# Prompt attention scores: two heads side by side on the halves of the contraction, in place of zero-padded queries

## The reference

```python
# group A (x = 0): chunk band, 8 chunks of 64 to the left, with a bias by distance
sc = jnp.einsum('bcqhd,bckhd->bchqk', chunked(q), k_band) * (d ** -0.5)
sc = jnp.where(valid, sc + bias, -jnp.inf)
o = jnp.einsum('bchqk,bckhd->bcqhd', jax.nn.softmax(sc), v_band)
# group B (x = 1): the 256 keys that an indexer scores highest, for each query
_, idx = lax.top_k(isc, k_sel)
sc = jnp.einsum('bqhd,bqkhd->bhqk', q, kg) * (q.shape[-1] ** -0.5)
o = jnp.einsum('bhqk,bqkhd->bqhd', jax.nn.softmax(sc), vg)
```

## Time and profile before

| | |
|---|---|
| median of 3 runs | 2865.4 us (2864.28 to 2867.36) |
| the profiled execution: its time, its span | 2869.77 us, 2866.3 us |
| PE busy, share of the span | 2603.8 us, 91% |
| PEld busy | 2326.6 us, 81% |
| DVE busy | 1359.8 us, 47% |
| ACT busy | 992.7 us, 35% |
| POOL busy | 632.3 us, 22% |
| mean granted clock of PE | 0.963 |
| first prompt score to the last but one tile's end | 1324.2 to 1673 us of the span |

### The profile page before, as it was taken

How to read it: one execution, slowest core, us unless ns; L and a number is a source line. 1 busy time by engine, 2 the same in 40 slices (tenths; PEclk the granted TensorE clock), 3 DMA queues, 4 the chain that set the end, 5 groups by cost and what they waited for, 6 DMA issues and landing times. The chain is left out here.

```text
span 2866.3 us, 39971 instructions
## 1 busy us (share of the span) xinstructions
PE 2603.8 (91%) x16468; PEld 2326.6 (81%) x16468; DVE 1359.8 (47%) x2369; ACT 992.7 (35%) x1691; POOL 632.3 (22%) x470
## 2 busy tenths in 40 slices
PE   2799999999998999986998989989299999999998
PEld 2799999988887799975776766658289999998886
DVE  6423333234543598986777723332523232333544
ACT  4333333333332323233666532221333333323332
POOL 5444333300001021831000000000633344320000
PEclk9899999999998999987999989999699999999999
DMA  2122122266542121213000334551011221227553
GB/s 88 41 82 78 61 78 72 88 229 218 209 142 64 49 95 63 78 51 120 23 31 30 111 105 167 178 190 45 22 61 63 91 78 61 78 68 264 187 205 145
DMA packets 153108, 294.26 MB, mean 103 GB/s; under 512 B 14032, under 2 KB 90456, under 8 KB 152928
## 3 DMA queue, kind: packets, MB, share of 16 engines
q1 hardware_dynamic: 146688, 268.12, 27.6%
q0 software_dynamic: 6240, 23.59, 2.2%
HBM read 237.26 MB, written 61.78 MB: 104 GB/s over the span
## 5 line engine op out<-in xcount | busy, mean ns | idle before, releaser
L720 DVE TENSOR_TENSOR f_dl<-f_raw_d,f_dh 128x2048 fp32r<-128x2048 f32 x66 | 151.3, 2293 | 274.1 <-ACT f_dh L568 274.1
L568 ACT ACTIVATE f_dh<-f_raw_d 128x2048 fp32r<-128x2048 f32 x66 | 126.5, 1916 | 321.6 <-PE f_pV L151 287.4
L149 PE MATMUL f_pX<-f_xop,f_g_shi 128*128 128x256 f32 (+1 forms) x528 | 159.4, 302 | 21.6 <-ACT f_gh L499 21.6
L499 ACT ACTIVATE f_gh<-f_pX 128x256 f32<-128x256 f32 (+1 forms) x132 | 54.1, 410 | 352.8 <-PE f_pX L151 352.7
L1897 PEld LDWEIGHTS t_po<-t_v,t_pT 128*128 128x128 f32 x1056 | 135.2, 194 | 33.8 <-DVE t_osb L1621 14.2
L150 PE MATMUL f_pX<-f_xop,f_g_shi 128*128 128x256 f32 (+1 forms) x528 | 158.5, 300 | 0.0
L151 PE MATMUL f_pX<-f_xop,f_g_slo 128*128 128x256 f32 (+1 forms) x528 | 158.4, 300 | 0.0
L1754 ACT ACTIVATE t_sc<-t_sc,t_small 128x640 f32<-128x640 f32 (+8 forms) x136 | 100.0, 735 | 165.8 <-DVE t_small L1682 130.2
L150 PE MATMUL f_pX<-f_xop,f_u_shi 128*128 128x256 f32 (+1 forms) x528 | 156.3, 296 | 0.0
L151 PE MATMUL f_pX<-f_xop,f_u_slo 128*128 128x256 f32 (+1 forms) x528 | 156.3, 296 | 0.0
L149 PE MATMUL f_pX<-f_xop,f_u_shi 128*128 128x256 f32 (+1 forms) x528 | 156.3, 296 | 0.0
(11 more groups left out here) (329 smaller groups left out, 8131.7 us busy)
## 6 DMA issues: line engine op xcount, KB each, us to landing
f_raw_d<-in_ffn_w_down SPq DMA_DIRECT2D x66, 1024.0 KB, 4.9
hid<-f_gh SPq DMA_DIRECT2D x22, 1152.0 KB, 8.8
f_raw_h<-hid SPq DMA_DIRECT2D x66, 384.0 KB, 5.5
f_g_raw<-in_ffn_w_gate SPq DMA_DIRECT2D x22, 1024.0 KB, 5.4
f_u_raw<-in_ffn_w_up SPq DMA_DIRECT2D x22, 1024.0 KB, 6.4
proj<-w_stage POOLq DMA_DIRECT2D x12, 1152.0 KB, 5.6
i_raw<-in_w_in SPq DMA_DIRECT2D x12, 1024.0 KB, 5.2
f_x<-in_x_prompt SPq DMA_DIRECT2D x16, 512.0 KB, 6.3
```

Of the source, the lines that this page charges most:

```text
L149: pe.matmul(out, a[0], b[0], start=first, stop=False, skip_group_check=goes_on)
L499: act.activation(dst, by_tile(pX[:, c, 0:N[c]]), ACT.Copy).then_inc(s_copy, 1)
L568: act.activation(d_hi[slot(q)][:], raw_d[slot(q)][:], ACT.Copy).then_inc(s_dhi, 1)
L720: dve.tensor_tensor(d_lo[slot(q)][:], raw_d[slot(q)][:], d_hi[slot(q)][:].bitcast(F32), ALU.subtract)
```

## The change

Queries are kept without zeros, two heads to a slice as the keys are. The scores of an even and an odd head are issued together, each a matmul over the 64 partitions of its head: for each four blocks first the even, then the odd head. The order becomes: behind `turn(g)` with g odd come `score(g + 1)` and `score(g + 2)`, behind an even one none. DVE and ACT walk the same list. The copy to `qT` is one of 128 partitions in place of two of 64, and the memset goes.

```diff
         plan.append(("turn", g))
-        if g + 2 < len(heads):
-            plan.append(("score", g + 2))
+        if g % 2 and g + 1 < len(heads):
+            plan += [("score", g + 1), ("score", g + 2)]
         if g >= 1:
             plan.append(("value", g - 1))
...
-        qT = keep("qT", [P, 2, H, P], F32)
+        qT = keep("qT", [P, 2, HT, P], F32)
...
-            pool.memset(qT[:], 0.0).then_inc(s_zero, 1)
...
-                    pool.wait_ge(s_zero, 3)
+                    pool.wait_ge(s_zero, 2)
...
-            act.wait_ge(s_zero, 1)
...
-                    for r in range(2):
-                        i = act.activation(qT[r * HD:(r + 1) * HD, n % 2, r::2, :],
-                                           pm[r * HD:(r + 1) * HD, :].rearrange("p (f c) -> p f c", c=P), ACT.Copy, scale=HD ** -0.5)
-                    i.then_inc(s_ma, 1)
+                    act.activation(qT[:, n % 2, :, :], pm[:].rearrange("p (f c) -> p f c", c=P), ACT.Copy, scale=HD ** -0.5).then_inc(s_ma, 1)
...
-                elif e[0] == "score":
+                elif e[0] == "score" and e[1] % 2 == 0:
...
                     if g >= 2:
-                        pe.wait_ge(s_mx, g - 1)
+                        pe.wait_ge(s_mx, g)
                     for c in range(0, nb, 4):
                         c1 = min(c + 4, nb)
-                        last = pe.matmul(ps[g % 2][:, c * P:c1 * P], qT[:, (x * NP + t) % 2, h, :],
-                                         kT[x][:, h // 2, (k0 + c) * P:(k0 + c1) * P], start=True, stop=True)
-                    last.then_inc(s_s, 1)
+                        for r in range(2):
+                            rs = slice(r * HD, (r + 1) * HD)
+                            last = pe.matmul(ps[r][:, c * P:c1 * P], qT[rs, (x * NP + t) % 2, h // 2, :],
+                                             kT[x][rs, h // 2, (k0 + c) * P:(k0 + c1) * P], start=True, stop=True)
+                            if c1 == nb:
+                                last.then_inc(s_s, 1)
```

## The result

The median went from 2865.6 to 2982.5 us (four executions each): ratio 1.0407, interval 1.0389 to 1.0425, +117 us. The forecast was slower, 2904, with a range to 2942: the sign was right and the size a third of what came. An execution over 1.5% longer than the fastest of its kernel is left out of ratios and medians; this concerns two of the four of one experiment, halves alone.

The account below looks back on a forecast made before the run. PE was taken to bound the kernel. Tiles of nb = 5 (+25 us) and the others (+3.8, +3.7, -2, +8.4) sum to +39: 2909 on the profiled execution, 2904 as median, range 2885 to 2942.

Parts of the forecast that it names:

- PE bounds the kernel before: Prompt attention loop: PE goes without a gap at nb = 5, 2.69 us a head, with slack of 1.5 us elsewhere.
- Overlap: Pair's scores on PE: only odd head's first record beside even head's second; 1.50 us for 2.14 at nb = 5, saving 34.
- The bound of 56 us of streaming: Upper bound on PE's saving from overlapping a pair's scores: half of all score streaming; 34 us was taken.
- the sum on PE: PE's score saving against array changes: -34 + 26 = -8 us; with full doubling 26 - 56 = -30.
- Array changes: PE going from 128 rows to 64 and back once a pair: 0.4 us each, 26 us for 64 pairs.
- Closed loop: Pair's chain through PE, DVE and ACT, no lookahead: 6.95 us at nb = 5 against 5.38; with overlap, chance 0.52.
- The sum: Change in prompt attention's time, tile by tile over all nb: +39 us, 2909 on the profiled execution.
- Prep: Preparing a tile at nb = 5: key copy stands behind the odd head's exponential; 2.1 us charged for `prep`.
- The clock: Rival: PE's idle gaps drop half the stretch to 1.2 GHz, about 0.7 us a pair, +45 us, 2949; chance 0.17.
- the two gaps of 1 us: PE's waits in a pair at nb = 5: some 0.8 us ahead of the even head's turn, 1.1 ahead of the odd's.
- my signs of being wrong: Odd head's turn starting without waiting, stretch clock under 0.9, or 64-row weight loads taking other than 0.19 us.
- the absence of overlap: Rival: the pair's score halves run one after the other, +23 us more at nb above 4: +62, 2927; chance 0.20.

Follow-up runs that it names:

- halves alone: The changed kernel with the old order, one head at a time in 64 rows: 3036 us from the two shorter executions, ratio 1.059.
- the two opened kernels: Early pair scores, key and query rows of `prep` separated, earlier `out`, output scaled between adds: 2817.6 us with 64-row halves, 2842.0 with zero-padded 128 rows.
- prep split: Kernel before, with `prep`'s query rows transposed behind the turn and next score, and no DVE select half at h = 2: 2840.5 us, 0.9914.
- the opened kernel with halves: Changed kernel with scores behind the even turn, `prep` in two parts, earlier `out`, output scaled between the adds: 2817.6 us, 0.9824.
- the small matmuls of 64 rows: Kernel before, with one matmul of 64 rows and 4 columns ahead of each head's scores: 2950.2 us, 1.0283.
- halves alone with prep split: One head at a time in 64 rows, old order, `prep`'s query rows later, no select half at h = 2: 3019.1 us, 1.0545.

## Why the prediction was wrong

- **PE bounds the kernel before**: right. Opening its waits made it faster; on DVE and ACT only the order of some work changed for it, not its amount.
- **Overlap**: right that there is one, too small. I let each head's second record wait its turn. The two heads' first records start 10 ns apart and so do the second ones, so a pair streams in the time of one head: 1.28 us with the change of the array at nb = 5 (forecast 1.50 + 0.2), 1.92 at nb = 8 (1776.53 to 1778.45, forecast 2.14 + 0.2). The bound of 56 us of streaming was the right value: with it and the 26 us of array changes the sum on PE is -30, and between the two opened kernels PE's busy time differs by 31 us (284.9 and 316.0). The Trainium skill, TensorE: Matmul & The Clock Gate, Part 3, says that small-contraction matmuls in distinct row groups run at once, and the trace agrees; the same section says that matmuls start and end in program order. For the matmuls as wholes the trace agrees with this too (the one of line 1877 starts first, at 1388.62, and its second record is the first of the two to end), but their records interleave: its second record (1389.15) starts 0.52 us after the first record of the matmul issued behind it (1388.63).
- **Array changes**, 0.4 us a round trip: right, 0.39 read off where whole scores stream through 64 rows and 0.28 where 4 columns do. The Trainium skill, TensorEngine Tiling (Array Packing), Key Properties, says that a change of tiling mode drains the array; the trace agrees in kind, but no row shows the drain by itself.
- **Closed loop**: right in place and order; 6.77 against 6.95 us. With 128 rows, prep split and a clock of 0.95 it costs 2892.7 - 2840.5 = 52 us over the old order with prep split, which has no select half at h = 2 besides; with prep whole the order costs 56. The sum had 39. (PE idle in 30% of the loop was a slip: by the sum's own 5.1 of 6.95 us it is 26%.)
- **Prep**: the step that failed in kind. I moved the key copy behind exponential b, charged 2.1 us for `prep` as before, and did not count the longer wait (35.2 us in all in place of 16.2) nor ask what else a single wait of 3 us does. Splitting `prep` takes away 25 us of this wait with halves and 20 with 128 rows, and gives 61 and 31 us.
- **The clock**: the term mis-sized. I had it as a rival with a chance of 0.17 and +45 us over the loop, all from the two gaps of 1 us. The sum itself had nothing for it, and the time came 78 us over the sum. PE's idle time in the prompt attention grew by 51 us (35.5 to 87.0), near the 47 that the sum implies (39, and 8 less work); PE's busy time should have fallen by 8 and grew by 64. The fall of the clock is enough for that: the opened kernel with halves has as many records and is busy 285 us at 0.97, the changed one 387 us at 0.76, 102 more. A clock under 0.9 in the stretch was among my signs of being wrong, and it came. Only in part are the gaps its cause: a kernel without them falls as well if one half of the array streams at a time (3019), and the loop with 128 rows stays at 0.95. What the changed kernel does is between: at nb = 5 it mostly holds 2.4 GHz through gaps of 0.8 us but not always (1520.56 above), loses it behind the 3 us of `prep`, and at nb = 1 to 3 stays low: clock 0.50 at 1345 to 1365. From the second tile's `prep` to the fifth's it takes 83.8 us (1356.16 to 1439.92) against 59.0 (1346.57 to 1405.54), +25 where the sum had some +7.
- **Range**: its upper end took the absence of overlap and a part of the clock's fall; my own rival of the clock, 2949 with a chance of 0.17, lay outside it. It left out that a wait costs more than its length where the clock falls behind it.

Shown by runs: the price of the order, of the wait in `prep`, of the array changes, and that with one half at a time PE can stay at 1.2 GHz without a wait where both halves at work bring it up. Only argued: why small tiles stay low in the changed kernel; the small matmuls of 64 rows, which did the same there, point to the array changes. Open: how the changed kernel's fall to 0.76 divides between its waits and its 64 rows, as no run has the one without the other at the same waits.

## What to carry to other kernels

Before pairing two items to save time on the bound engine, draw the loop of one pair through every engine's own order: a lookahead of two single items is not one of a pair, and what stands between the two on the other engines enters the loop in full. Packing two halves pays here only together with the order that feeds it (2818 against 2842 padded and 2983 as changed). A matmul on one half of the array alone should be charged with the clock too: padding it with zeros was faster by 179 us (3019 against 2840).

## What the runs showed of the hardware

- Two float32 matmuls on separate halves, issued one behind the other, run record by record side by side, 10 ns apart.
- With one half at work at a time (halves alone with prep split) PE went at 1.2 GHz without a single wait (clock 0.50, busy 50.00 of 50; from 1562 to 1742 us of the span 180.00 of 180), and in another window of the same kernel at 2.4 GHz with the same kind of work. With both halves at work (nb = 3 and 4) the clock was 1.00 where it had been 0.50. A half-used array kept the level it came with for long stretches; what decides between the two was not settled, and executions of halves alone differ by 85 us (3025 to 3111).
- Adding matmuls whose result is not used made a kernel some 120 us faster (3036 to 2916).
- A change of the array from 128 to 64 rows and back cost 0.39 us of PE's time around a score of 640 columns and 0.28 around 4 columns, at 2.4 GHz.
- Behind waits of 0.80 and 0.86 us, 2.1 us apart, the clock was once found at 1.2 GHz (1520.56); behind the same waits it mostly stayed at 2.4.
